# Normed rows of chunks 5 to 9 turned by way of DRAM and VectorE instead of TensorE

## The reference

```
h = rmsnorm(x, mix_norm)                       # x * rsqrt(mean(x^2) + eps) * gain
[aq ak av | z xbc dt | mq mk mv mo mi mf] = split(h @ w_in)      # 1024 x 2848
x = x + concat(window_attention, bidirectional_ssd, bidirectional_mlstm) @ w_out
x = x + expert_choice_swiglu_moe(rmsnorm(x, ffn_norm))
```

## Time and profile before

| | |
|---|---|
| median of three runs | 2242.45 us |
| the profiled execution | 2246.58 us, its span 2245.1 us |
| TensorE busy | 2219.8 us (99%) |
| VectorE, ScalarE, GpSimd busy | 1235.4, 617.7, 564.9 us |
| share of TensorE in the chain that ended last | 89% |

### The profile page before, as it was taken

The page is one execution under the profiler, slowest core; times in us unless marked ns, Lnnn a source line. Parts: engine busy times, 40 slices in busy tenths (PEclk is TensorE's granted clock), DMA queues, the critical chain, the costliest instruction groups (busy, mean ns, idle before and its releaser), DMA issues.

```text
span 2245.1 us, 32479 instructions
## 1 busy us (share of the span) xinstructions
PE 2219.8 (99%) x12464; PEld 1581.4 (70%) x12464; DVE 1235.4 (55%) x2404; ACT 617.7 (28%) x1421; POOL 564.9 (25%) x660
## 2 busy tenths in 40 slices
PE   9999999999999999999999999999999999999998
PEld 7557578874446888877775575888744468877786
DVE  3555466586765445554236554665867654555442
ACT  4221233474332111111132212334743311111111
POOL 1104455154311111111111044541442111111111
PEclk9999999999999999999999999999999999999999
DMA  4002122633657988888440021335346579878883
GB/s 160 21 20 76 57 94 94 164 115 126 211 182 269 339 294 292 278 275 290 141 131 21 21 75 56 99 107 134 113 145 203 191 277 351 281 272 299 291 290 74
DMA packets 179540, 388.84 MB, mean 173 GB/s; under 512 B 12181, under 2 KB 63897, under 8 KB 179386
## 3 DMA queue, kind: packets, MB, share of 16 engines
q1 hardware_dynamic: 162042, 344.68, 44.5%
q0 software_dynamic: 15264, 41.95, 7.6%
q10 hardware_dynamic: 2080, 0.13, 0.1%
HBM read 329.77 MB, written 56.96 MB: 172 GB/s over the span
## 4 chain that ended last, share of the span: by engine, by line
PE 89%; DVE 4%; ACT 2%; DMA 2%; issue 1%; POOL 0%; SPq 0%; DVEq 0%; ACTq 0%; POOLq 0%
PE ps L1989 87%; DVE TMP L1799 1%; DMA MID<-w_up 1%; PE ps L2015 1%; ACT SCR L1138 1%; DMA HT<-h_sample,idxs 1%; DVE SCR L1804 1%; DVE TMP L1804 0%; PE ps L2048 0%; DMA MID<-x_sample 0%; DVE HT L1360 0%; DVE HT L1931 0%; DVE TMP L1360 0%; ACT RING L1138 0%; DMA HT<-h_prompt,idxg 0%
## 5 line engine op out<-in xcount | busy, mean ns | idle before, releaser
L1989 PE MATMUL ps<-MID,HT 128*128 128x512 f32 (+3 forms) x2560 | 679.8, 490 | 1.8 <-DVE HT L1360 1.2
L1989 PEld LDWEIGHTS ps<-HT,MID 128*128 128x128 f32 x4096 | 555.4, 191 | 16.7 <-issue 15.0
L1989 PE MATMUL ps<-HT,MID 128*128 128x160 f32 (+1 forms) x4096 | 558.8, 298 | 1.2 <-DVE HT L1360 0.9
L1989 PEld LDWEIGHTS ps<-MID,HT 128*128 128x128 f32 (+1 forms) x2560 | 298.6, 156 | 284.9 <-issue 246.7
L1989 PE MATMUL ps<-RING,HT 128*128 128x256 f32 (+2 forms) x1760 | 387.3, 389 | 0.0
L1989 PEld LDWEIGHTS ps<-RING,HT 128*128 128x128 f32 (+1 forms) x1760 | 313.0, 190 | 59.9 <-issue 17.4
L1989 PE MATMUL ps<-HT,RING 128*128 128x512 f32 (+1 forms) x960 | 349.8, 522 | 0.0
L1989 PEld LDWEIGHTS ps<-HT,RING 128*128 128x128 f32 x960 | 180.2, 190 | 153.3 <-issue 145.2
L1931 DVE STREAM_TRANSPOSE HT<-HT 32x256 f32<-32x256 f32 x576 | 251.1, 436 | 18.4
L1369 DVE SCALAR_TENSOR_TENSOR HT<-HT,ps 128x160 f32<-128x160 f32 (+1 forms) x128 | 40.8, 319 | 396.9 <-ACT HT L1322 394.9
L932 POOL DMA_INDIRECT y_prompt<-SCR,idxp x32 | 50.3, 1573 | 584.0 <-ACT SCR L1332 543.2
(11 more groups left out here) (287 smaller groups left out, 2113.0 us busy)
## 6 DMA issues: line engine op xcount, KB each, us to landing
MID<-w_gate SPq DMA_DIRECT2D x32, 2048.0 KB, 8.9
MID<-w_up SPq DMA_DIRECT2D x32, 2048.0 KB, 14.8
MID<-w_down SPq DMA_DIRECT2D x32, 2048.0 KB, 15.3
RING<-w_in SPq DMA_DIRECT2D x20, 1024.0 KB, 5.3
SCR<-cs_rows SPq DMA_DIRECT2D x20, 1024.0 KB, 5.1
p_rows<-SCR SPq DMA_DIRECT2D x12, 768.0 KB
HT<-p_rows SPq DMA_DIRECT2D x48, 192.0 KB, 3.5
y_sample<-RING SPq DMA_DIRECT2D x16, 512.0 KB, 4.3
```

What stands on the lines that cost most here:

```text
L1989: return pe.matmul(out, a, b, start=start, stop=stop)
```

## The change

Chunks 0 to 4 are made as before. For chunks 5 to 9 (XB = 5) VectorE multiplies the rows by root and gain at once (`weigh_x`, four instructions into one of three buffers XP), SyncE stores them to a DRAM tensor x_norm_rows (`x_store`), four DMAs load their blocks back into XN[c] (`x_blocks`), and VectorE transposes the blocks into hT (`turn_x` of VectorE). The gain must then lie along the row on all partitions: TensorE spreads it by eight products with a broadcast column (`spread_gains`) into banks 3 and 4, and ScalarE copies it to GAINS. TensorE's turn_x(2), which writes bank 4, waits for that copy. On SyncE each chunk's blocks are asked for behind its own store and the next chunk's store; ring slice 1 follows the blocks of chunk 8 and slice 2 those of chunk 9. ScalarE takes the reads of the first zg units later, behind more of the squares.

More of the change, by code:

```diff
@@ L112, with ht_at @@
 BY_ROWS = (0, 1, 2, NC - 1)
+XB = 5
+X_STORED = 16 * (NC - XB)
+def ht_at(c):
+    return 2 * c + 2 if c < XB else XB + c + 1
 def turned_for(n):
@@ L513, in counts @@
         def counts(layer):
-            return {"x": 16 * layer, "scatter": 16 * E * layer, "halves": 16 * (E + 1) * layer,
+            return {"x": 16 * layer, "par": 16 * (layer + 1) + 64 * len(range(XB + 1, NC, 2)) * layer,
+                    "blocks": [16 * (layer + 1) + 64 * len(range(XB + 1, NC, 2)) * layer, 16 + 64 * len(range(XB, NC, 2)) * layer], "scatter": 16 * E * layer, "halves": 16 * (E + 1) * layer,
                     "gather": [16 * layer * len(range(j, E, 3)) for j in range(3)],
@@ L586, in _ @@
                         x_load(c)
-                    ring_load(1)
+                    def x_store(c):
[5 more added lines that the diff above has]
+                        rows = xnr[(c - XB) * P:(c - XB + 1) * P, :]
+                        for b in range(4):
+                            sp.dma_start(XN[c][32 * b:32 * b + 32, :].rearrange("p (a w) -> p a w", a=4),
[3 more added lines that the diff above has]
+                        sp.wait_ge(scratch_stored, 16 * (c - XB + 1))
+                        if c + 1 < NC:
+                            x_store(c + 1)
+                        x_blocks(c)
+                        if c == NC - 2:
+                            ring_load(1)
                     ring_load(2)
@@ L1027, in _ @@
                     square(1)
-                    for c in range(2, NC):
+                    square(2)
+                    square(3)
+                    scale_x(2)
+                    act.wait_ge(ht_made, 5)
+                    link(act.copy(GAINS[:, 0:512], ps[:, 3, :]))
+                    link(act.copy(GAINS[:, 512:1024], ps[:, 4, :]), softplus_exp)
+                    square(4)
+                    square(5)
+                    evac(0)
+                    scale_x(4)
+                    for c in range(6, NC):
                         square(c)
[L1030 to L1033, removed]
+                        evac(c - 5)
+                    evac(NC - 5)
+                    evac(NC - 4)
                     for u in range(NC - 3, NC):
                         evac(u)
-                    act.wait_ge(par_loaded, 16 * (layer + 1))
+                    act.wait_ge(par_loaded, seen["par"])
                     link(act.activation(NEGA, pr("alog"), ACT.Exp), softplus_exp)
@@ L1378, in _ @@
                         link(dve.memset(IDLE, 0.0), first_scaled)
-                    dve.wait_ge(par_loaded, 16 * (layer + 1))
+                    dve.wait_ge(par_loaded, seen["par"])
                     def scale_x(c):
@@ L1401, in _ @@
                         if c == 3:
+                            weigh_x(XB)
                             scale_first()
+                            weigh_x(XB + 1)
+                    weigh_x(XB + 2)
+                    for c in range(XB, NC):
+                        turn_x(c)
+                        if c + 3 < NC:
+                            weigh_x(c + 3)
                     dve.wait_ge(cst_loaded, 16)
@@ L2013, in turn_x @@
                                 pe.wait_ge(ht_copied, 2 * c - 3 + j)
+                            if c == 2 and j == 0:
+                                pe.wait_ge(softplus_exp, 1)
                             for k in range(4):
@@ L2023, in unit @@
                             pe.wait_ge(zg_loaded, 48 * (layer + 1))
-                            pe.wait_ge(ht_copied, 2 * g + (1 if k1 <= KD // 2 else 2))
+                            pe.wait_ge(ht_copied, ht_at(g) - (1 if k1 <= KD // 2 else 0))
                         else:
@@ L2050, in turn_xs, with spread_gains @@
                             last.then_inc(xs_turned, 1)
+                    def spread_gains():
+                        pe.wait_ge(par_loaded, seen["par"])
+                        for k in range(KD):
+                            last = mm(ps[:, 3 + k // 4, k % 4 * P:(k % 4 + 1) * P], pr("gmix")[:, k:k + 1].to_broadcast([P, P]), ident)
+                        last.then_inc(ht_made, 1)
                     turn_x(0)
@@ L2059, in _ @@
                     turn_x(1)
+                    spread_gains()
                     if layer > 0:
                         unit(1)
-                    for c in range(2, NC):
+                    for c in range(2, XB):
                         turn_x(c)
@@ L2065, in _ @@
                             unit(c - 1)
-                    unit(NC - 1)
+                    for c in range(XB - 1, NC):
+                        unit(c)
                     def xbc(f, g0=0, g1=3):
@@ L2385, in _ @@
                     turn_qk(1)
-                    pe.wait_ge(scaled, 4 + (NC - 2) // 2)
+                    pe.wait_ge(scaled, 4 + len(range(2, XB, 2)))
                     out_proj(0, 0, 0, 2)
```

24 lines of the change are left out of this document (15 added, 9 removed).

## The result

The changed kernel took 2249.33 us (median of 9 runs, 2246.18 to 2255.05), the kernel before 2242.22 (9 runs); the ratio is 1.003 with a 95% interval of 1.0021 to 1.0038. I had forecast 2238.5 and a range of 2235.0 to 2245.5. The two profiled executions don't show this by themselves: 2246.32 us after against 2246.58 before. Three more traces of the changed kernel and two of the one before tell why; they stand at the end of the experiments.

The account below looks back on a forecast made before the run. TensorE, busy 99% of the span, was taken as the bound. The terms -8.7 + 2.3 + 0.5 + 0.7 + 1.1 + 0.1 = -4.0 us took the median from 2242.45 to 2238.5 us, range 2235.0 to 2245.5.

Parts of the forecast that it names:

- What goes: Start of each layer: TensorE no longer turns chunks 5 to 9, 4.35 us less a layer, 8.7 in both.
- The gains: Spreading and copying gains ahead of chunk 2's turning: 2.3 us more in layer 0, 0.5 more in layer 1.
- 0.1 in all: Layer 0, chunk 9: blocks behind ring slice 1, turned at 53.25 and wanted at 53.36; 0.1 us late in layer 1.
- 1.9: Ring slice 1 ahead of chunk 9's blocks adds 1.9 us, from a slice's landing of 5.3 and a block's of 3.4.
- The trip of 5.4: Chunks 5 to 9: first block's issue to last landing takes 5.4 us, 1.3 for issuing plus 4.1 for landing.
- have half a microsecond or more to spare: Layer 0: chunk 6 turned at 39.95, wanted at 40.6; chunk 8 at about 48.7, wanted at 49.5; no wait.
- Layer 1's low clock: Head of layer 1: the low clock behind the gap ahead of chunk 3 remains, unit 2 taking 5.57 us, 1.7 extra.
- the slack that I gave chunk 5: Layer 1: slow unit 2 gives slack, chunk 5 turned at 1153.95 and wanted at 1155.0, so wait 0.
- a rival: Rival 3: the clock falls in layer 0 behind the new gap of 1.45 us, giving 2240.1; chance 0.08.
- The rival that came: Rival 2: the round trip sets the pace through VectorE's in-order loop from a trip of 6.3 us; 2247 to 2252, chance 0.17.
- its sign: Sign of rival 2 in the profile after: units 6 or 8 wait as well.
- The rule against the row: Skill page's estimate, 2.3 us a block and 3.2 a store, no waits, against rows of 3.4 or more and 2.9.

Follow-up runs that it names:

- Without the trip: Changed kernel without stores and block loads of the normed rows, raw rows transposed, ring slices behind the loads of x: 2239.42 us against 2243.55 before, ratio 0.9982.
- the run with TensorE kept busy: Changed kernel with idle products ahead of unit 9, four in layer 0, two in layer 1: 2248.9 us against 2242.16 before, ratio 1.0027.
- weighing ahead: Changed kernel with VectorE's weighing of chunk c + 3 ahead of the transpose of chunk c: 2249.51 us against 2243.52 before, ratio 1.0028.
- the slices are last: Changed kernel with ring slice 1 moved behind the blocks of chunk 9, slice 2 following: 2242.03 us against 2243.52 before, ratio 0.9997.

## Why the prediction was wrong, step by step

- **What goes: right.** Without the trip, layer 0 is 2.1 earlier, which is 4.35 less 2.3.
- **The gains: right in layer 0** (chunk 2 at 17.95, forecast 17.9 to 18.0; +2.4 us alone in the medians). In layer 1 the 0.5 holds in the first trace, where chunk 2 didn't wait for the copy. In the other three traces it waited 0.8 to 1.1, and 2.9 in the run with TensorE kept busy. The first trace had its low clock at unit 0, so TensorE came later; in the others it came earlier and found square 3 ahead of the copy. That order was not tested by itself.
- **The step that failed: chunk 9's "0.1 in all".** The wait was 2.7 in layer 0 and 1.7 in layer 1, up to 4.7 in other executions, and putting the slice one chunk later gave back 7 us. In layer 0 chunk 9 was turned at 57.46 and not 53.25, which is 4.2 late. Three terms make that up:
  - 1.5 for the slice ahead. I priced it at 1.9, the difference of two landings; chunk 9's trip took 3.4 more than chunk 8's (2.3 in layer 1; 3.3 in the mean of the four traces).
  - 2.1 for the start of the trip, at 46.82 and not 44.7. Weighing 9 ended at 43.0 and not near 41.8, and SyncE then issued store 9, four blocks and the slice, 3.7 us, before it came to chunk 9. I had only the landing of store 9 in between.
  - 0.6 for the trip without a slice, 6.0 and not 5.4.

  TensorE came 1.5 later than forecast, which leaves the 2.7. The sum had also left out that these blocks wait for the transpose of chunk 7, which I had at 45.6, later than my 44.7; in layer 0 that ended at 46.13 and did not decide. The order of the queue was right.
- **Why 1.9 was too small.** A difference of landings takes out a fixed part that is in both; that is an argument, and no run here separates it. In the 9 us behind chunk 9's first issue the queues moved 275 GB/s in the mean, so 1 MB is 3.8 us, an estimate from that rate; in six of the eight cases (four traces, two layers) it is nearer to the measured difference than 1.9.
- **The trip of 5.4: 0.3 too short in the mean.** For chunks 5 to 8 it measured 5.2 to 6.2 in the first trace. The landings were as taken (3.2 to 4.3 against 4.1), but from the first to the fourth issue it took 1.8 to 2.2 us and not 1.3.
- **Chunks 6 and 8 "have half a microsecond or more to spare": wrong for 8**, which made unit 8 wait 0.85 and 0.76. The 48.7 for chunk 8 holds the same loop (39.95 + 1.8 + 0.4 + 5.4 + 1.25), but starts from chunk 6 turned at 39.95. Chunk 6 was turned at 41.30, after a trip of 6.2, and chunk 8's trip took 6.0.
- **Layer 1's low clock: there behind chunk 3 in three of the four traces.** In those unit 5 waited 0.2 or less, as forecast. In the first trace it came at unit 0, unit 2 took 3.88 and not 5.57, the slack that I gave chunk 5 was not there, and unit 5 waited 1.0. I had read the low clock behind a gap of 1.93 from one trace; with the same gaps the other two traces of the kernel before kept the full clock (unit 2 took 3.88).
- **The low clock behind the waits**, which I priced only in a rival, belongs to the forecast once a wait is as long as these.
- **The rival that came** is the second (2247 to 2252, chance 0.17), and its sign, a wait ahead of unit 8, came too. But it was to decide by a trip of 6.3 or more in the loop, and of the 32 trips of chunks 5 to 8 in the four traces one was that long (6.8); and weighing ahead shows that the loop gives back 1.8 in the medians once the slices are last, and nothing while a slice stands ahead of chunk 9.
- **The rule against the row.** In the first trace the blocks without a slice ahead landed in 3.2 to 4.3, so the row was again the better guide. The Trainium skill, "DMA: Bandwidth & Descriptors", section "Anatomy of one DMA", gives for the GpSimd path about 2.0 us plus the bytes at 436 GB/s; the estimate by it is 2.3 for a block. That is 1.8 below the 4.1 that I took for a landing, not the 1.5 that I wrote.

Open: why the slice ahead of chunk 9 was slow in one execution, and how much of an ordinary run's loss each low stretch holds.

## What to carry to other kernels

When a transfer on the path is put on a queue that other transfers share, price what stands ahead of it as its bytes at the rate of that stretch, which came nearer here than a difference of landing times, add the time that the issuing engine needs for everything in between, and put what is wanted later behind it. In a loop through several in-order engines, carry the lateness of each chunk on to the next ones, and look for the instruction that could stand ahead of the one that waits. One trace of each kernel can hide a loss of 0.3%: here they differed by 0.3 us where the medians differed by 7.

## What the runs showed of the hardware

Four block loads of 128 KB that SyncE issued within 1.3 us, first start to last, in rows 7 took 1.8 to 2.2 in the first trace of the changed kernel, each set right behind the issue of a 512 KB store or of a ring slice. A slice of 1 MB issued just ahead of four such loads made their trip 9.4 instead of 6.0 in layer 0, and one issued just behind them changed nothing (9.35 without it). The kernel before has the same gaps of 1.2 and 1.93 us at the head of layer 1 in all three traces; behind the second the granted clock was 0.50 in the first trace and 1.00 in the other two, so the length of that gap alone didn't decide it.
